# The value sums of the sample group's cached attention: weights held in the array and cached values moved through it, in place of the other way round

## The chip, the core and the metric

The kernel runs on one core of a Trainium2 chip. The time is that of one execution on the device, in microseconds (us); the profile is of another execution of the same program, taken by the hardware profiler. TensorE (PE) multiplies: a matmul has a stationary operand that is loaded first (PEld) and a moving operand that is then passed through it, column by column. VectorE (DVE), ScalarE (ACT) and GpSimd (POOL) work on elements; SyncE (SP) issues all DMAs of this kernel. PE writes to PSUM, which has eight banks of 512 fp32 numbers in each of 128 partitions.

## What is computed

The reference is one inference step of a decoder trunk with two layers (DEPTH = 2), for a prompt of 1024 tokens and for 8 sample sequences of one new token each. Half of each layer's 16 heads are window attention in three patterns (window, dilation), and for the sample group these heads read 2048 cached positions:

```
def dilated_gather_stats(q, k_all, v_all, window, dilation, buf_len):
    ...
    kg = jnp.take(k_all, idxc, axis=1).astype(jnp.float32)
    vg = jnp.take(v_all, idxc, axis=1).astype(jnp.float32)
    s = jnp.einsum('bthd,btjhd->bthj', q.astype(jnp.float32), kg) * (HEAD_DIM ** -0.5)
    ...
    o = jnp.einsum('bthj,btjhd->bthd', e, vg) / l[..., None]
    return m, l, o
```

The three patterns are merged by their softmax denominators. For each of 8 sequences b and 8 heads h the result is thus a sum over 3 x 128 cached values of 64 numbers, with one weight for each value, and over the new token's own value. The other eight heads are a matrix memory (mLSTM) that goes through the prompt in eight chunks of 128 tokens. Both halves are normalised, multiplied by w_out and added to x; then come a gated convolution block and a per-layer embedding.

## The kernel before

Each layer runs in stages: the input projection w_in in eight pairs of heads (`products`), each pair's projection lying beside the work of the pair before it; attention for pairs 0 to 3; the mLSTM for pairs 4 to 7; the output projection; the feed-forward block; the embedding. A hand-written order fixes what stands on each engine, and semaphores join the engines. Large products are made of three fp32r matmuls on split halves (lines 779 to 781); the small ones of attention and mLSTM are plain f32, and each of these shows as two matmul records in the trace.

The change lies in the last mLSTM pair (`q + 1 == PAIRS`), where no projection is left to lie beside it, and in what follows up to the output projection.

The mLSTM loop has eight steps c. On PE a step is: `sample_values(c)`; three products of the chunk (lines 1063, 1073, 1076); `kq(c + 1)` (line 994). On DVE it is: `finish(c)` (its first line is 1871, and it waits for PE's line 1076); `prepare(c + 1)`, which PE's lines 1063 and 1073 of the next step wait for; `output_gate(c)`; and a piece of the sample group's work: `sample_weights` at c = 0, `sample_turned` at 1, nothing at 2, `memory_gates` at 3, `memory_keys` at 4, `memory_output` at 5, `memory_update` at 6.

A tile i = 3b + r is 128 cached positions (pattern r of sequence b) by 512 numbers (8 heads by 64). `load_values(i)` brings one, `value_place(i)` is where it lies, in the space of the split operands `hi` and `lo` (trace name of the first: cache, of the second: vectors). The softmax weights are turned so that positions lie on partitions, and copied to `pT` (line 1764). At steps 2 to 7 `sample_values` takes four tiles each: for each quarter of a tile it loads 128 columns of values as the stationary operand and moves the 8 columns of weights (the 8 heads) of that b and r through it, which gives every head's weights times every value column (line 1011). Only the part with equal heads is wanted: eight copies of 8 columns pick it (`oT`, line 1936), before DVE normalises the first rows of y (`normalise`, line 1950).

After the loop, `normalise(t)` scales 128 tokens, `turn_y(t)` (line 1103) turns them on PE, `y_high` (ACT, line 1432) and `y_low` (DVE, line 1978) split them, and from t = 2 on the output projection can start. Behind its first product PE turns `oT` back (line 1089), DVE copies it to `so`, and two DMAs through DRAM bring it to the layout of `sv`.

SP issues DMAs in one order: 22 value tiles, then a wait for `rb_ready`, gains, half of X, two tiles of y, a store of the last output gate and a wait for it, its load, then tiles 22 and 23, each behind a count of `v_used`, then a wait for `mem_done` (the end of `memory_update`), the memory's stores and further y tiles.

## Time and profile before

| what | value |
|---|---|
| median of 3 runs | 3680.07 us (3679.55 to 3680.49) |
| the profiled execution | 3673.24 us, of it 3671.4 us from first to last instruction |
| PE busy | 3358.6 us (91%) |
| DVE busy | 2168.9 us (59%) |
| mean granted clock of PE | 0.934 of 2.4 GHz |

The table is of the whole run, and a change of one stage has to be read from that stage. The profile splits time by groups of instructions, by stretches (busy time of each engine and granted clock between two times), and in order of time. A granted clock of 1.00 is 2.4 GHz and one of 0.50 is 1.2 GHz. An engine's idle time stands in square brackets before the instruction that ended it, with what released it. Layer 1 of the two has the place in question at 770 to 852 us, layer 2 about 1803 us later.

### The profile page before, as it was taken

How to read it: one execution, taken by the hardware profiler on the slowest of the kernel's cores; microseconds unless marked ns; L12 is line 12 of the kernel's file. 1: busy time of each engine (PE TensorE's matmuls, PEld its weight loads, DVE VectorE, ACT ScalarE, POOL GpSimd, SP SyncE). 2: the span in 40 equal slices, each digit the busy share in tenths (PEclk: the TensorE clock that was granted, in tenths of full speed). 3: DMA queues.
4: the chain of work that ended last, by engine and by line, in shares of the span. 5: the costliest groups of instructions: out<-in, count | busy, mean ns of one | idle time of the engine just before them, and what ended most of it. 6: DMA issues, size and time to landing. Idle time of an engine off the chain costs nothing. (4 is left out here: it accounts for less than half of the span.)

```text
span 3671.4 us, 49568 instructions
## 1 busy us (share of the span) xinstructions
PE 3358.6 (91%) x19817; PEld 3084.5 (84%) x19817; DVE 2168.9 (59%) x4644; ACT 883.5 (24%) x1661; POOL 600.5 (16%) x498
## 2 busy tenths in 40 slices
PE   4888999988999999999978889997799999999989
PEld 4777767677899999998977777675798999999989
DVE  5566446657655555557566664566566555555573
ACT  4233223212311111113232323223032111111131
POOL 2001102110221221221110011111003221221211
PEclk7999989958999999999989999898599999999999
DMA  4111112343111111110211111134311111111101
GB/s 139 39 36 41 38 38 74 81 137 79 58 47 47 47 48 45 57 48 18 83 50 32 45 40 41 37 95 114 121 49 50 35 58 47 35 58 47 38 29 62
DMA packets 208269, 209.69 MB, mean 57 GB/s; under 512 B 34596, under 2 KB 180964, under 8 KB 205936
## 3 DMA queue, kind: packets, MB, share of 16 engines
q1 hardware_dynamic: 208040, 206.53, 18.7%
q8 instruction: 157, 2.57, 0.3%
q14 instruction: 72, 0.59, 0.1%
HBM read 175.03 MB, written 31.64 MB: 56 GB/s over the span
## 5 line engine op out<-in xcount | busy, mean ns | idle before, releaser
L763 POOL TENSOR_TENSOR wlo<-raw,whi 128x512 fp32r<-128x512 f32 (+3 forms) x488 | 599.8, 1264 | 3013.3 <-ACT whi L1251 3013.3
L779 PE MATMUL ps<-hi,wlo 128*128 128x344 f32 x2880 | 931.6, 323 | 25.7 <-DVE wb L2071 15.5
L780 PE MATMUL ps<-lo,whi 128*128 128x344 f32 x2880 | 925.0, 321 | 0.0
L781 PE MATMUL ps<-hi,whi 128*128 128x344 f32 x2880 | 924.6, 321 | 0.0
L779 PEld LDWEIGHTS ps<-hi,wlo 128*128 128x128 f32 x2880 | 546.2, 190 | 29.0 <-DVE wb L2071 16.1
L780 PEld LDWEIGHTS ps<-lo,whi 128*128 128x128 f32 x2880 | 545.5, 189 | 0.6
L781 PEld LDWEIGHTS ps<-hi,whi 128*128 128x128 f32 x2880 | 545.7, 189 | 0.0
L779 PE MATMUL ps<-whi,lo 128*128 128x512 f32 (+5 forms) x1152 | 463.0, 402 | 43.9 <-POOL wlo L763 25.6
L780 PE MATMUL ps<-wlo,hi 128*128 128x512 f32 (+5 forms) x1152 | 441.5, 383 | 0.0
L781 PE MATMUL ps<-whi,hi 128*128 128x512 f32 (+5 forms) x1152 | 441.3, 383 | 0.0
L2083 DVE TENSOR_TENSOR X<-X,ps 128x344 f32<-128x344 f32 x528 | 268.4, 512 | 196.1 <-PE ps L781 195.5
L779 PE MATMUL ps<-yhi,wlo 128*128 128x344 f32 x1056 | 339.8, 322 | 0.7 <-DVE X L2083 0.6
L781 PE MATMUL ps<-yhi,whi 128*128 128x344 f32 x1056 | 338.2, 320 | 0.0
L780 PE MATMUL ps<-ylo,whi 128*128 128x344 f32 x1056 | 337.3, 319 | 0.0
L779 PEld LDWEIGHTS ps<-whi,lo 128*128 128x128 f32 (+1 forms) x1152 | 216.6, 188 | 114.8 <-issue 58.4
L1477 ACT ACTIVATE wb<-wb 128x344 f32<-128x344 f32 x132 | 64.9, 492 | 848.9 <-DVE wb L2054 848.9
L781 PEld LDWEIGHTS ps<-whi,hi 128*128 128x128 f32 (+1 forms) x1152 | 215.7, 187 | 41.2 <-issue 3.6
L780 PEld LDWEIGHTS ps<-wlo,hi 128*128 128x128 f32 (+1 forms) x1152 | 216.6, 188 | 35.1 <-issue 3.0
L1251 ACT ACTIVATE whi<-raw 128x2048 fp32r<-128x2048 f32 (+3 forms) x122 | 214.0, 1766 | 52.1 <-DMA raw<-in_w_down 40.0
L1299 ACT ACTIVATE zt<-ps,rcol 128x256 f32<-128x256 f32 x144 | 68.0, 472 | 597.5 <-PE ps L781 460.6
L1705 DVE COPY att<-ps 128x512 f32<-128x512 f32 (+3 forms) x128 | 75.7, 591 | 221.6 <-PE ps L906 221.3
L779 PEld LDWEIGHTS ps<-yhi,wlo 128*128 128x128 f32 x1056 | 198.7, 188 | 2.1 <-DVE X L2083 1.5
(273 smaller groups left out, 4333.9 us busy)
## 6 DMA issues: line engine op xcount, KB each, us to landing
raw<-in_w_up SPq DMA_DIRECT2D x44, 1024.0 KB, 5.0
raw<-in_w_in SPq DMA_DIRECT2D x112, 256.0 KB, 4.4
raw<-in_w_down SPq DMA_DIRECT2D x22, 1024.0 KB, 4.7
kvb<-in_cache_win_k SPq DMA_DIRECT2D x48, 256.0 KB, 3.1
cache<-in_cache_win_v SPq DMA_DIRECT2D x36, 256.0 KB, 5.7
x_scratch<-X SPq DMA_DIRECT2D x8, 1032.0 KB, 6.9
X<-x_scratch SPq DMA_DIRECT2D x4, 2064.0 KB, 15.0
raw<-in_w_out SPq DMA_DIRECT2D x8, 1024.0 KB, 6.5
```

Source lines behind the costliest of these rows:

```text
L763: pool.tensor_tensor(out=wlo[:, s, r], in0=raw[:, s, r], in1=whi[:, s, r].bitcast(F32), op=ALU.subtract).then_inc(w_split, 1)
L779: nc.tensor.matmul(out, a_lo, b_hi, start=first, stop=False)
L780: nc.tensor.matmul(out, a_hi, b_lo, start=False, stop=False)
L781: return nc.tensor.matmul(out, a_hi, b_hi, start=False, stop=last)
L1251: do(nc.scalar.activation(whi[:, s, 0:used], raw[:, s, 0:used], ACT.Copy), w_hi, wait=False)
L1299: do(nc.scalar.activation(zt[0:m, z, t, 0:2 * P], src[:, 0:2 * P], ACT.Identity, scale=r), wait=False)
L1477: do(nc.scalar.activation(wb[:, col(c)], wb[:, col(c)], ACT.Gelu_apprx_tanh), gelu_done, wait=False)
L1705: do(v.tensor_copy(att[:, a:a + n], ps[:, 4, 0:n]), pt0, wait=False)
L2083: do(v.tensor_tensor(out=x, in0=x, in1=ps[:, 5 + g % 3, 0:CH], op=ALU.add), dn_read, wait=False)
```

## The change

The operands change places. A tile of values is now the moving operand, 512 columns; the stationary operand is 64 columns of `pZ`, one for each (b, h), in which only the 8 columns of this tile's b hold weights and the others are zero. So all 24 tiles add into one bank, 64 partitions (b, h) by 512 columns, with one matmul for a tile. `pZ` takes the place of three value tiles, so SP loads 19 tiles ahead and 5 behind counts of `v_used`. `pZ` is set to zero at the end of `sample_weights`, and `sample_turned` makes three copies with gaps in place of one. A table `heads` of zeros and ones (64 x 8, one more small DMA) picks the own head: one product of 64 x 512 out of PSUM, then a sum over heads straight into `sv`. Both stand right behind `normalise(0)`. The eight `oT` copies, the turn on PE, the copy to `so` and the two DMAs are gone; PE's third product of the output projection, which uses the same bank, waits for `so_done`.

```diff
         Cs, Ct = [lof[:, j * 2048:(j + 1) * 2048].rearrange("p (v k) -> p v k", k=HD) for j in (0, 1)]
         sm = lof[0:HD, 7168:7168 + 385]
-        pT = lof[:, 7560:7560 + 3 * HD]
+        pZ = lof[:, 5632:5632 + 3 * WA]
+        sown = lof[0:HD, 4096:4096 + WA].rearrange("p (h d) -> p h d", h=NH)
         zb = lof[0:HD, 7760:7760 + 3 * HD].rearrange("p (s d) -> p s d", s=3)
         small = lof[0:HD, 7960:7960 + 16]
 
...
         def value_place(i):
 
-            if 16 <= i < 22:
-                return lof[:, 4096 + (i - 16) * WA:4096 + (i - 15) * WA]
-            return hif[:, (i % 22) * WA:(i % 22 + 1) * WA]
+            s = i % 19
+            if s >= 16:
+                return lof[:, 4096 + (s - 16) * WA:4096 + (s - 15) * WA]
+            return hif[:, s * WA:(s + 1) * WA]
...
-                for i in range(22):
+                for i in range(19):
                     load_values(i)
                 sp.wait_ge(*at(rb_ready, 2 * PAIRS))
+                sp.dma_start(heads[:, :], A["c_heads"]).then_inc(ygain_in, 16)
                 for h, name in enumerate(("out_norm_a", "out_norm_b")):
                     sp.dma_start(rowr[:, h * WA:(h + 1) * WA], A[name][l:l + 1, :].to_broadcast([P, WA])).then_inc(ygain_in, 16)
                 sp.dma_start(X[:, 0:4, :], Xd[:, 0:4, :]).then_inc(x_back[0], 16)
...
                 sp.wait_ge(*at(z_stored[1], stored_value(last)))
                 sp.dma_start(mz[:, 2 * HD + 32:3 * HD], Zd[6].rearrange("b (r d) -> (b r) d", d=32)).then_inc(mo_in, 16)
-                for i in (22, 23):
-                    sp.wait_ge(*at(v_used, i - 21))
+                for i in range(19, 24):
+                    sp.wait_ge(*at(v_used, i - 18))
                     load_values(i)
                 sp.wait_ge(*at(mem_done, 1))
...
                 for t in (6, 7):
                     sp.wait_ge(*at(yt_ready, t - 3))
                     load_y(t)
-                sp.wait_ge(*at(so_done, 1))
-                sp.dma_start(Ad, so[:, :]).then_inc(as_stored, 16)
-                sp.wait_ge(*at(as_stored, 16))
-                sp.dma_start(sv[:, 1, :], Ad.rearrange("b (h d) -> (b h) d", d=HD)).then_inc(as_in, 16)
                 sp.wait_ge(*at(mh_stored, 32))
...
                         for i in range(4 * c - 8, 4 * c - 4) if c >= 2 else ():
                             b, r = divmod(i, 3)
+                            a = r * WA + b * HD
                             pe.wait_ge(*at(v_in[i // 6], 96))
-                            for x in range(4):
-                                mm = nc.tensor.matmul(ps[:, 6, x * HD + b * NH:x * HD + (b + 1) * NH], value_place(i)[:, x * P:(x + 1) * P],
-                                                      pT[:, r * HD + b * NH:r * HD + (b + 1) * NH],
-                                                      start=(r == 0 and x == 0), stop=(r == 2 and x == 3))
-                            mm.then_inc(v_used, 1)
+                            nc.tensor.matmul(ps[0:HD, 6, :], pZ[:, a:a + HD], value_place(i), start=(i == 0), stop=(i == 23)).then_inc(v_used, 1)
...
-                def turn_sample():
-
-                    pe.wait_ge(*at(ot_done, 1))
-                    for c in range(4):
-                        mm = nc.tensor.transpose(ps[0:NB, 7, c * P:(c + 1) * P], oT[:, c, :], ident[:, :])
-                    mm.then_inc(so_ready, 1)
...
-                        if j >= 3:
+                        if j == 2:
+                            pe.wait_ge(*at(so_done, 1))
+                        elif j >= 3:
                             pe.wait_ge(*at(wo_done, j - 2))
                         for k in range(KT):
                             w_h, w_l = weights(B + B_OUT + o // 2, k, 256, (o % 2) * P, P)
                             mm = three(ps[:, 4 + j % 3, 0:CH], w_h, w_l, hi[:, k, col(c)], lo[:, k, col(c)], k == 0, k == KT - 1)
                         mm.then_inc(gemm_done, 1)
-                        if c == 0 and o == 0:
-                            turn_sample()
                         if c == 0 and o + 3 < NT:
                             turn_y(o + 3)
                         if c == 1 and o == 3:
...
                     do(v.tensor_scalar(sv[:, 0, :], zb[:, 2, :], sm[:, 384:385], None, ALU.mult))
+                    do(v.memset(pZ, 0.0))
 
                 def sample_turned():
+
                     dve.wait_ge(*at(pj_back, 1))
-                    do(v.tensor_copy(pT, ps[:, 7, 0:3 * HD]), pj_done)
+                    for r in range(3):
+                        src = ps[:, 7, r * HD:(r + 1) * HD].rearrange("p (b h) -> p b h", b=NB)
+                        own = lof[:, 5632 + r * WA:5632 + r * WA + NB * (HD + NH)].rearrange("p (b x) -> p b x", b=NB)[:, :, 0:NH]
+                        do(v.tensor_copy(own, src), pj_done if r == 2 else None, wait=False)
...
                 rsqrt(yrs[:, :], yt2[:, :], ssq[:, :], WA, None)
-                dve.wait_ge(*at(v_used, 3 * NB))
-                for c in range(4):
-                    for e in range(2):
-                        r = slice(HD * e, HD * e + HD)
-                        src = ps[r, 6, c * 64:(c + 1) * 64].rearrange("p (b h) -> p b h", h=NH)[:, :, 2 * c + e]
-                        do(v.tensor_copy(oT[r, c, :], src), ot_done if (c, e) == (3, 1) else None, wait=False)
-                dve.wait_ge(*at(ygain_in, 32))
+                dve.wait_ge(*at(ygain_in, 48))
...
                 def sample_out():
-                    dve.wait_ge(*at(so_ready, 1))
-                    do(v.tensor_copy(so[:, :], ps[0:NB, 7, :]), so_done)
+
+                    dve.wait_ge(*at(v_used, 3 * NB))
+                    do(v.tensor_tensor(out=sown, in0=ps[0:HD, 6, :].rearrange("p (h d) -> p h d", h=NH),
+                                       in1=heads[:, :].unsqueeze(2).to_broadcast([HD, NH, HD]), op=ALU.mult), so_done)
 
                 def sample_sum():
-                    dve.wait_ge(*at(as_in, 16))
+                    do(v.tensor_reduce(out=sv[:, 1, :], in_=sown.rearrange("p h d -> p d h"), axis=AX.X, op=ALU.add))
                     do(v.tensor_tensor(out=sv[:, 0, :], in0=sv[:, 0, :], in1=sv[:, 1, :], op=ALU.add), sa_done)
...
                 normalise(0)
+                sample_out()
+                sample_sum()
                 for t in range(3):
                     normalise(t + 1)
                     if t == 0:
@@ -2008,10 +1997,6 @@
                             y_low(o + 3)
                         if c == 0 and o % 4 == 0:
                             dve.wait_ge(*at(x_back[o // 4], 16))
-                        if c == 0 and o == 1:
-                            sample_out()
-                        if c == 0 and o == 5:
-                            sample_sum()
                         if c == 1 and o == 1:
                             sample_norm()
                             normalise(NT)
...
-    return {"c_ident": ident, "c_mask": mask, "c_causal": causal, "c_rope": rope}
+    heads = np.equal(np.arange(HD)[:, None] % NH, np.arange(NH)[None, :]).astype(f)
+    return {"c_heads": heads, "c_ident": ident, "c_mask": mask, "c_causal": causal, "c_rope": rope}
```

On PE, in two steps of the loop over the last pair, before:

```order
L1011 MATMUL ps<-vectors,cache 128x8 x16
L1063 MATMUL ps<-zt,att 128x130
L1073 MATMUL ps<-zt,att 128x65 x2
L1076 MATMUL ps<-Cst,att 128x130
L994 MATMUL ps<-rstd,kT 128x128 x2
```

and with the change:

```order
L1007 MATMUL ps<-cache,vectors 64x512 x4
L1056 MATMUL ps<-zt,att 128x130
L1066 MATMUL ps<-zt,att 128x65 x2
L1069 MATMUL ps<-Cst,att 128x130
L990 MATMUL ps<-rstd,kT 128x128 x2
```

The 16 matmuls of four tiles became four, with 512 columns each in place of 8; nothing else of the step moved.

On DVE, between the end of the reciprocal root over all rows and the first split of y (vectors is the space where `sown` lies), before:

```order
L1548 TENSOR_TENSOR yrs<-yrs,yt 128x18
L1936 COPY oT<-ps 64x8 x8
L1950 SCALAR_TENSOR_TENSOR kvb<-kvb,yrs,rowr 128x512
L1950 SCALAR_TENSOR_TENSOR kvb<-kvb,yrs,rowr 128x384
L1950 SCALAR_TENSOR_TENSOR kvb<-yb,yrs,rowr 128x128
```

and with the change:

```order
L1534 TENSOR_TENSOR yrs<-yrs,yt 128x18
L1935 SCALAR_TENSOR_TENSOR kvb<-kvb,yrs,rowr 128x512
L1935 SCALAR_TENSOR_TENSOR kvb<-kvb,yrs,rowr 128x384
L1935 SCALAR_TENSOR_TENSOR kvb<-yb,yrs,rowr 128x128
L1942 TENSOR_TENSOR vectors<-ps,heads 64x512
L1946 TENSOR_REDUCE sv<-vectors 64x64
L1947 TENSOR_TENSOR sv<-sv 64x64
```

Eight short copies ahead of `normalise(0)` are gone, and three instructions stand between it and `normalise(1)`.

On SP, around the value tiles, before:

```order
L588 DMA cache<-in_cache_win_v 128x512 x16
L588 DMA vectors<-in_cache_win_v 128x512 x6
```

and with the change:

```order
L587 DMA cache<-in_cache_win_v 128x512 x16
L587 DMA vectors<-in_cache_win_v 128x512 x3
L657 DMA heads<-in_c_heads 64x8
```

The other three tiles went to where tiles 22 and 23 are loaded, behind the load of the last output gate.

## Rows read from the trace of the kernel before

**Rows 1.** The page's first line.

```profile
span 3671.4 us, 49568 instructions
```

**Rows 2.** Stretch: us, each engine's busy time (count), granted clock, DMA share, GB/s.

```profile
781.03:828.89 47.86, 47.72 (x220) 45.38 (x220) 28.69 (x75) 0.21 (x1) 0.00 (x0) 0.50 0.04 14
```

**Rows 3.** PE in order of time: start, duration, instruction, count; one step.

```profile
781.55 6.99 PE L1011 MATMUL ps<-vectors,cache 128*128 128x8 f32 x32
788.39 0.78 PE L1063 MATMUL ps<-zt,att 128*128 128x130 f32 x2
...
791.12 6.99 PE L1011 MATMUL ps<-vectors,cache 128*128 128x8 f32 x32
```

**Rows 4.** DVE in order of time: first line of `finish`, steps 1 to 7.

```profile
767.93 0.60 DVE L1871 SCALAR_TENSOR_TENSOR Cst<-Cst,cwb,ps 64x65 f32<-64x65 f32 x2 [1.63 <-PE ps L1076]
...
781.03 0.60 DVE L1871 SCALAR_TENSOR_TENSOR Cst<-Cst,cwb,ps 64x65 f32<-64x65 f32 x2 [9.12 <-PE ps L1076]
...
790.61 0.60 DVE L1871 SCALAR_TENSOR_TENSOR Cst<-Cst,cwb,ps 64x65 f32<-64x65 f32 x2 [6.28 <-PE ps L1076]
...
800.18 0.60 DVE L1871 SCALAR_TENSOR_TENSOR Cst<-Cst,cwb,ps 64x65 f32<-64x65 f32 x2 [4.06 <-PE ps L1076]
...
809.75 0.60 DVE L1871 SCALAR_TENSOR_TENSOR Cst<-Cst,cwb,ps 64x65 f32<-64x65 f32 x2 [2.92 <-PE ps L1076]
...
819.33 0.60 DVE L1871 SCALAR_TENSOR_TENSOR Cst<-Cst,cwb,ps 64x65 f32<-64x65 f32 x2 [2.89 <-PE ps L1076]
...
828.89 0.60 DVE L1871 SCALAR_TENSOR_TENSOR Cst<-Cst,cwb,ps 64x65 f32<-64x65 f32 x2 [0.95 <-PE ps L1076]
```

**Rows 5.** PE in order of time: 512-column f32 matmuls at either clock, and line 1063.

```profile
548.37 0.38 PE L1063 MATMUL ps<-zt,att 128*128 128x130 f32 x2
...
672.57 3.69 PE L1048 MATMUL ps<-rowr,ident 8*128 8x512 f32 x8
...
743.16 7.19 PE L1048 MATMUL ps<-rowr,ident 8*128 8x512 f32 x8
```

**Rows 6.** PE in order of time: two short runs at the lower clock.

```profile
358.92 2.93 PE L891 MATMUL ps<-zt 64*128 64x512 f32 x8 [2.75 <-DVE nm L1696]
...
496.10 3.17 PE L965 MATMUL ps<-ident,gz 128*8 128x128 f32 x16 [0.74 <-DVE yb L1713]
```

**Rows 7.** Stretches as in Rows 2: around those two runs, and two others.

```profile
358.90:362.10 3.20, 2.93 (x8) 1.17 (x8) 3.03 (x8) 0.99 (x2) 0.00 (x0) 0.50 0.26 82
362.30:366.00 3.70, 3.70 (x28) 3.66 (x29) 1.67 (x4) 1.59 (x4) 0.00 (x0) 1.00 0.00 0
...
495.30:498.60 3.30, 2.56 (x13) 1.52 (x13) 2.73 (x6) 0.00 (x0) 0.00 (x0) 0.50 0.29 84
498.80:502.00 3.20, 3.20 (x18) 2.64 (x16) 2.58 (x5) 0.00 (x0) 0.00 (x0) 1.00 0.66 238
...
743.20:750.30 7.10, 7.10 (x10) 2.44 (x8) 1.58 (x3) 2.18 (x8) 0.00 (x0) 0.50 0.97 75
851.70:857.00 5.30, 5.24 (x18) 5.24 (x19) 1.46 (x4) 0.00 (x0) 0.00 (x0) 0.50 0.60 53
```

**Rows 8.** The page's DMA issues: count, KB each, median us to landing.

```profile
cache<-in_cache_win_v SPq DMA_DIRECT2D x36, 256.0 KB, 5.7
```

**Rows 9.** Groups of DVE instructions: busy time and mean ns; or shortest, median, longest ns.

```profile
L1843 DVE TENSOR_TENSOR att<-ps,causal 128x512 f32<-128x512 f32 x32 | 20.6, 686 | 3.5 <-PE ps L1048 3.1
...
L1814 DVE MEMSET kT<- x2: 912/912/912, 497.9 to 2300.7; 8x1024 f32 x2
```

**Rows 10.** In order of time, behind the loop: DVE and PE.

```profile
838.92 1.52 DVE L1936 COPY oT<-ps 64x8 f32<-64x8 f32 x8
...
844.90 1.29 DVE L1978 TENSOR_TENSOR lo<-ps,hi 128x512 fp32r<-128x512 f32 x2 [1.43 <-ACT hi L1432]
...
842.16 3.64 PE L1103 MATMUL ps<-ident,kvb 128*128 128x128 f32 x16 [11.98 <-DVE kvb L1950]
...
858.05 0.60 PE L1089 MATMUL ps<-ident,oT 128*8 128x128 f32 x4
```

More of the change, by code:

```diff
@@ L210 @@
 PER = dict(
-    w_hi=NBLK, w_split=NBLK * PIECES, gemm_done=GEMM_ALL, vec_in=32, x_spilled=64, x_back0=16, x_back1=16, ygain_in=32,
+    w_hi=NBLK, w_split=NBLK * PIECES, gemm_done=GEMM_ALL, vec_in=32, x_spilled=64, x_back0=16, x_back1=16, ygain_in=48,
     split_hi=72, split_lo=72, sq_ready=72, sq_used=72, ss_ready=9, rstd_done=9, rcol_ready=3, rcol_done=3,
@@ L218 @@
     c_stored=192, zb_in=48, mz_in=208, mo_in=16, kq_used=24, st_ready=1, sp_max=1, sp_exp=1, pj_ready=1, pj_back=1, pj_done=1,
-    k_in0=192, k_in1=192, v_in0=96, v_in1=96, v_in2=96, v_in3=96, q_in0=64, q_in1=64, v_used=24, ot_done=1, so_ready=1, so_done=1,
-    as_stored=16, as_in=16, sc_exp_in=1, sc_exp=1, sa_done=1, sa_stored=16, mem_done=1, mh_stored=32, cst_in=16, cst_out=48,
+    k_in0=192, k_in1=192, v_in0=96, v_in1=96, v_in2=96, v_in3=96, q_in0=64, q_in1=64, v_used=24, so_done=1,
+    sc_exp_in=1, sc_exp=1, sa_done=1, sa_stored=16, mem_done=1, mh_stored=32, cst_in=16, cst_out=48,
     ys_in=48, yt_ready=9, yn_done=9, yh_done=18, yl_done=18, yst_in0=32, yst_in1=32, yst_in2=32, yst_in3=32, wo_done=24,
@@ L318, in build @@
         sv = sb("sv", [HD, 2, HD], F32, mid)
-        oT = sb("oT", [P, 4, NB], F32, mid)
-        so = sb("so", [NB, WA], F32, mid)
+        heads = sb("heads", [HD, NH], F32, mid)
         mz = sb("mz", [P, 3 * HD], F32, mid)
@@ L353, in build @@
         Hd = nc.dram_tensor("h_scratch", [NB, WA], F32).ap()
-        Ad = nc.dram_tensor("a_scratch", [NB, WA], F32).ap()
         ident_in, const_in, const_set = sem("ident_in"), sem("const_in"), sem("const_set")
@@ L390, in build @@
         q_in = [sem(f"q_in{s}") for s in range(2)]
-        v_used, ot_done, so_ready, so_done, as_stored, as_in, sc_exp_in, sc_exp = [sem(n) for n in (
-            "v_used", "ot_done", "so_ready", "so_done", "as_stored", "as_in", "sc_exp_in", "sc_exp")]
+        v_used, so_done, sc_exp_in, sc_exp = [sem(n) for n in ("v_used", "so_done", "sc_exp_in", "sc_exp")]
         sa_done, sa_stored, mem_done, mh_stored = sem("sa_done"), sem("sa_stored"), sem("mem_done"), sem("mh_stored")
```

## Prediction

> **What bounds the kernel now.** I read three views of the last mLSTM pair of layer 1: busy time by stretch, then PE and DVE in order of time. The stretch from `finish(2)` to `finish(7)` is 47.86 us; PE is busy for 47.72 of them and DVE for 28.69, at a granted clock of 0.50, the 1.2 GHz level [rows 2]. So PE sets the pace, and PE alone. A step is 9.57 us: 6.84 from the first matmul of four value tiles to line 1063 (781.55 to 788.39), and 2.73 for the chunk's products and `kq` (788.39 to 791.12) [rows 3]. The 6.99 us for 32 records are 0.218 each for 8 moving columns: what takes this time is the load of 128 columns, not the moving. DVE's first line of `finish` waits for PE in each step, by 9.12, 6.28, 4.06, 2.92, 2.89 and 0.95 us [rows 4]. Step lengths less these waits are what DVE itself needs: 9.58 - 6.28 = 3.30 us from `finish(2)` to `finish(3)`, then 9.57 - 4.06 = 5.51, 9.57 - 2.92 = 6.65, 9.58 - 2.89 = 6.69 and 9.56 - 0.95 = 8.61. Whatever PE gives back, a step can't go below these. Behind the loop the order turns: PE waits 11.98 us for `normalise` [rows 10], and DVE sets the end.
>
> **The matmuls.** Four tiles take four f32 matmuls, 8 records, of 512 columns. The nearest row is line 1048, also f32 and 512 columns: 8 records in 7.19 us at the low clock and in 3.69 us at the high one [rows 5], with one last pipeline tail in each; between starts I count 0.85 and 0.43. So four tiles cost 6.8 us at 1.2 GHz, what they cost now, and 3.4 us at 2.4 GHz. The exchange of operands gains nothing by itself. All hangs on the clock.
>
> **The clock.** Rows that speak for a rise: eight f32 records of 512 columns ran at 0.50 from 358.92, and the clock was 1.00 at 362.30; they were pairs of 64-row matmuls, two heads side by side [rows 6, 7]. Sixteen f32 records of 128 columns, with all 128 rows in use but only 8 stationary columns, ran at 0.50 from 496.10, and it was 1.00 at 498.80 [rows 6, 7]. So few stationary columns do not keep it down, and the new form (128 rows, 64 stationary columns, 512 moving) lies between those two. Against it: line 1048 kept PE busy for 7 us and the clock stayed at 0.50 [rows 7]. Its rows are 8 of 128, which the new form's aren't. Now, PE passes few columns in these steps, and the clock never moves. I take it that the clock rises about 3 us (3.4 and 2.7 in the two cases) after step 2's value tiles start, and holds: behind it PE is busy for 4.9 us of each step of 5 to 8.6.
>
> The Trainium skill, TensorE: Matmul & The Clock Gate, PE-mode transpose, says the full clock does not engage for transposes, since they do not count as busy in the same way. Line 965 is a transpose, and the clock rose behind it, so the trace does not bear this rule out here. The same page, Back-to-back issue gap, gives N / 1.2 ns at the cold clock, 427 ns for 512 columns; an estimate by that page would be 1.7 us for four tiles even without a rise, and DVE would then bound all steps and the gain would be near that of the forecast. The f32 rows show 0.85 us a record and two records a matmul, so the sum does not go by it.
>
> **The loop, per layer.** At the high clock a PE step is 3.4 + 2.73 / 2 = 4.8, with a little for hand-overs 4.9 us (line 1063 shows the halving: 0.78 us at the low clock, 0.38 at the high) [rows 3, 5]. A step is the longer of PE's and DVE's: 4.9, 5.51, 6.65, 6.69, 8.61, together 32.4 us, against 47.86: 15.5 less. Before `finish(2)`, step 2's tiles run 3 us at the low clock and the rest in half the time, and the products halve: 1.9 + 0.7 = 2.6 less if it is quick, nothing if the clock rises just behind the step; I take 1.9. Setting `pZ` to zero: 1536 columns at the rate of line 1814 (1024 in 0.912) are 1.4 us [rows 9], up to twice that beside POOL's work; it stands ahead of `finish(1)`, which now waits 1.63 us for PE [rows 4], so 0 to 1.2 shows; I take 0.4. Three copies of 64 columns in place of one of 192 are 0.3 us more, and PE waits for them. Loop: 15.5 + 1.9 - 0.7 = 16.7 less.
>
> **Behind the loop, per layer.** Eight `oT` copies, 1.52 us [rows 10], are gone from DVE's path, and `normalise(0)` comes 1.5 earlier. Added behind it: a product of 64 x 512 out of PSUM, 0.69 as line 1843 [rows 9], a sum with a stride, bounded by 0.5 and 1.4, taken as the product's 0.69, and an add, 0.2: 1.6 us. They shift `normalise(1)` back to where it was, but the first `y_low` waits 1.43 us today for ACT [rows 10], which waits for the first turn on PE; that turn is now earlier, so this wait closes. What is late next is `y_low(1)`, by the same turn: I count 1.1 less at the first product of the output projection, between -0.5 and 1.5. Line 1089's turn, 0.60 us with its tail [rows 10], goes from a PE-bound stretch: 0.4. The `so` copy, two DMAs and the earlier `sv` were waited for by nobody. Sum: 1.5 less.
>
> **SP.** Tiles 19 to 23 wait for counts 1 to 5 of `v_used`; the fifth comes early in step 3. Their landing takes 5.7 us each in the median [rows 8], and step 6 needs them some 17 us later (three steps): no cost. Queued behind these waits is only the wait for `mem_done`, which ends later. The memory's stores and the y tiles then start with `mem_done`, which comes right ahead of `finish(7)` where it came 0.95 us ahead; the y tiles are thus up to 0.9 nearer to their use. I cost that at nothing, at most 0.9. `heads` is 2 KB, long there.
>
> **Sum.** (16.7 + 1.5) x 2 = 36.4 us less. On the profiled execution's 3673.2 us (its span is 3671.4 [rows 1]) that is 3636.8; the median lies 6.8 above the profiled execution, so 3643.7. Unknown within it: where the clock stands when the output projection starts (it runs at 0.50 for 5.3 us now [rows 7], half of which can be gained or added, 2.7 a layer), the stretch before `finish(2)` (+0.7, -1.9), the zeroing (+0.4, -0.8), the tail (+0.4, -1.6). Taken together, not all at one end: 3634 to 3652.
>
> **Rivals.**
> 1. The clock stays at 1.2 GHz, since only 8 of 64 loaded columns are not zero, or by what keeps it down in line 1048. Then the loop is as now (6.8 against 6.84 for four tiles), less the 0.7 of added DVE work, and only the tail is won: 2 x (1.5 - 0.7) = 1.6 less, 3678.5. For: nothing has raised it in these steps so far. Against: lines 891 and 965. If transposes did not count, as the page has it, half of this evidence would fall, and this is the case that it would lead to.
> 2. The clock rises but falls back once DVE is the bound and PE waits some 2 to 3 us in steps 5 to 7, and steps run partly at the low clock. A step on PE at the low clock is 9.57, against 6.65 to 8.61 for DVE: 1 to 3 lost for each such step, 3 to 4 for steps 3 and 4. Three to five of them in each layer are 4 to 9 us: 3652 to 3662.
> 3. Slower: the clock stays low, and the weight loads are not hidden behind moving columns of the same rows. A load of 128 columns is 0.218 us [rows 3], one of 64 between half and all of that; 48 of them in each layer are 10 to 21 us over both layers. Taking the upper, 3678.5 + 21 = 3699.5. It decides from 0.08 us shown on each record (48 x 2 x 0.08 = 7.7 us). Against: the records of line 1048 stand end to end with their loads beneath them.
> 4. The change doesn't do what it says to PE's wait: tiles 19 to 23 come late and PE waits for them in step 6, up to 10 us a layer: 3645 to 3664.
>
> **How the numbers follow.** Forecast 0.74, rival 1 0.10, rival 2 0.10, rival 3 0.03, rival 4 0.03. Predicted: 3643.7. The range reaches from 3634 over rival 2 to 3662: 0.86 less what the forecast has outside its own bounds. A measurement of this kernel can tell about 0.2%, 7.4 us, from no change. Faster: forecast, rivals 2 and 4: 0.87. Same: rival 1: 0.10. Slower: 0.03.
>
> **What would show it.** The value matmuls at 0.85 us a record at first and 0.43 behind step 2; the granted clock 1.00 from step 3; DVE without waits from `finish(4)` on, 32 us from `finish(2)` to `finish(7)`; DVE idle less than 0.3 us before the first `y_low`. A clock of 0.50 through the stretch would prove the forecast wrong, and steps of over 10 us with it would mean rival 3.

## The result

The changed kernel takes 3643.22 us in the median of four runs (3641.94 to 3645.54), the kernel before, run beside it, 3680.28 us (3679.55 to 3680.98). The ratio is 0.9896, with a 95% interval of 0.9884 to 0.9908: 37.1 us less. Forecast were 3643.7 us and 36.4 us less.

The profiled execution of the changed kernel took 3642.27 us:

```profile
span 3640.5 us, 48964 instructions
PE 3315.6 (91%) x19521; PEld 3007.9 (83%) x19521; DVE 2170.7 (60%) x4636; ACT 883.6 (24%) x1661; POOL 600.6 (16%) x498
```

PE is busy for 43.0 us less than before and DVE for about as long as before. The stretches, in layer 1, are those of [rows 2] and [rows 7] moved to the same instructions: from `finish(1)` to `finish(2)`, on to `finish(7)`, on to the first product of the output projection, then two parts of the second stretch. Columns: us, busy time of PE, PEld, DVE, ACT and POOL (count), granted clock, DMA share, GB/s.

```profile
772.93:784.77 11.84, 7.51 (x22) 2.88 (x22) 4.46 (x14) 0.00 (x0) 3.14 (x3) 0.61 0.90 350
784.77:817.51 32.74, 25.69 (x100) 11.36 (x98) 28.70 (x76) 0.21 (x1) 0.00 (x0) 0.93 0.13 41
817.51:839.33 21.82, 6.51 (x26) 4.89 (x26) 20.69 (x49) 3.58 (x6) 0.00 (x0) 0.50 0.84 233
777.72:782.00 4.28, 4.28 (x5) 1.21 (x6) 0.00 (x0) 0.00 (x0) 0.00 (x0) 0.50 0.97 408
782.40:812.80 30.40, 28.06 (x111) 12.66 (x109) 24.07 (x74) 0.21 (x1) 0.00 (x0) 1.00 0.17 57
```

The second row answers to [rows 2]: 32.74 us for 47.86, at a clock of 0.93 for 0.50. DVE does the same 28.7 us of work in it and is now the busier engine. The fourth and fifth row show the clock: 0.50 until 782, then 1.00. The value matmuls in order of time on PE (start, duration, engine, line, operation, count; in brackets the idle time before) answer to [rows 3]:

```profile
777.72 5.84 PE L1007 MATMUL ps<-cache,vectors 128*64 128x512 f32 x8 [4.33 <-DVE vectors L1755]
785.00 3.65 PE L1007 MATMUL ps<-cache,vectors 128*64 128x512 f32 x8
788.58 0.49 PE L1056 MATMUL ps<-zt,att 128*128 128x130 f32 x2
790.09 3.65 PE L1007 MATMUL ps<-cache,vectors 128*64 128x512 f32 x8
```

Four tiles take 5.84 us in step 2, across the rise, and 3.65 behind it, where they took 6.99; a step of PE is 790.09 - 785.00 = 5.09 us, where it was 9.57. DVE's first line of `finish` for steps 1 to 7, which answers to [rows 4]:

```profile
772.93 0.60 DVE L1862 SCALAR_TENSOR_TENSOR Cst<-Cst,cwb,ps 64x65 f32<-64x65 f32 x2
784.77 0.60 DVE L1862 SCALAR_TENSOR_TENSOR Cst<-Cst,cwb,ps 64x65 f32<-64x65 f32 x2 [7.10 <-PE ps L1069]
789.88 0.60 DVE L1862 SCALAR_TENSOR_TENSOR Cst<-Cst,cwb,ps 64x65 f32<-64x65 f32 x2 [1.82 <-PE ps L1069]
795.43 0.60 DVE L1862 SCALAR_TENSOR_TENSOR Cst<-Cst,cwb,ps 64x65 f32<-64x65 f32 x2
802.13 0.60 DVE L1862 SCALAR_TENSOR_TENSOR Cst<-Cst,cwb,ps 64x65 f32<-64x65 f32 x2
808.85 0.60 DVE L1862 SCALAR_TENSOR_TENSOR Cst<-Cst,cwb,ps 64x65 f32<-64x65 f32 x2
817.51 0.60 DVE L1862 SCALAR_TENSOR_TENSOR Cst<-Cst,cwb,ps 64x65 f32<-64x65 f32 x2
```

The waits of 4.06, 2.92, 2.89 and 0.95 us are gone. The bound has passed from PE to DVE at `finish(4)`, and DVE keeps it.

Where the time went, by the same instructions in both traces (the first column is from the start of one to the start of the next):

| stretch, us | before, layer 1 / 2 | after, layer 1 / 2 |
|---|---|---|
| `finish(0)` to `finish(2)` | 22.92 / 22.93 | 20.90 / 21.47 |
| `finish(2)` to `finish(7)` | 47.86 / 47.85 | 32.74 / 32.74 |
| `finish(7)` to first output product | 22.87 / 22.66 | 21.82 / 21.83 |
| sum | 93.65 / 93.44 | 75.46 / 76.04 |

That is 18.2 and 17.4 us less. The turn at line 1089 of the kernel before is gone too (0.44 us in each layer, start to start), and the output projection runs at the low clock for 4.3 us in place of 5.3 in layer 1, which is worth 0.5. Together 37.0 us by these terms, and 37.1 by the medians. The two spans differ by only 30.9, since the profiled execution of the kernel before was a quick one: it starts `finish(0)` of layer 1 at 758.11, the changed kernel at 763.87, with the same instructions on PE and DVE up to there. From `finish(0)` to the end the two traces differ by 36.7, so the terms explain the difference to 0.3 us.

### The profile page after: what moved, and what is told of

Same layout as the page of the kernel before. It is cut to its first block and busy times, and to the rows that moved or that the text cites. A ratio compares the mean times of both kernels' runs of the same rounds, so it can differ in the third digit from the quotient of the medians.

```text
span 3640.5 us, 48964 instructions
## 1 busy us (share of the span) xinstructions
PE 3315.6 (91%) x19521; PEld 3007.9 (83%) x19521; DVE 2170.7 (60%) x4636; ACT 883.6 (24%) x1661; POOL 600.6 (16%) x498
```

## Experiments: what raised the clock

**Fewer rows.** The theory of the prediction was that line 1048 left the clock at 0.50 because it uses 8 of 128 rows. Here each value matmul uses 32 rows, and 96 of the 128 positions of a tile are left out.

```diff
-nc.tensor.matmul(ps[0:HD, 6, :], pZ[:, a:a + HD], value_place(i), ...)
+nc.tensor.matmul(ps[0:HD, 6, :], pZ[0:32, a:a + HD], value_place(i)[0:32, :], ...)
```

> The changed kernel, but each value matmul uses only rows 0 to 31 of its tile: 96 of the 128 positions of a tile are left out of the sum. Instructions, columns and waits are the same as in the changed kernel. Theory (the clock rose because these matmuls use all 128 rows; line 1048, 512 columns on 8 rows, left it at 0.50): the granted clock stays at 0.50 from finish(2) to finish(7) in layer 1, the eight value records of each step stay 0.85 us apart, a step is about 9.6 us, and the time is that of the kernel before less the tail, 3676 to 3681 us. Rival (512 moving columns a matmul and a busy PE are enough, whatever the rows): clock 1.00 from the second step on, 3641 to 3646 us.

Measured: 3679.21 us, ratio to the kernel before 0.9993 (0.9984 to 1.0003). The stretch from `finish(2)` to `finish(7)`, then two rows of PE's first step in it:

```profile
791.51:840.35 48.84, 48.68 (x100) 19.43 (x100) 28.71 (x76) 0.21 (x1) 0.00 (x0) 0.50 0.06 23
```

```profile
792.05 7.08 PE L1007 MATMUL ps<-cache,vectors 32*64 32x512 f32 x8
799.07 0.80 PE L1056 MATMUL ps<-zt,att 128*128 128x130 f32 x2
```

The same instructions, with PE busy for 48.68 of 48.84 us, leave the clock at 0.50. The rows in use, and with them the positions that enter the sum, are the only difference, so the theory stands. The run also shows the exchange of operands without its clock: a stretch of 48.84 us against 47.86, that is a loss of 1.0, which the shorter tail gives back. So nearly all of the 37 us hangs on the clock.

**Half the rows.** The same edit with `0:64`; half the positions of a tile are left out.

> The changed kernel, but each value matmul uses only rows 0 to 63 of its tile: half the positions of a tile are left out of the sum. With 32 rows the clock stayed at 0.50 and the time was 3679.2 us; with 128 it rises and the time is 3643 to 3645 us. Theory (rows in use count, in proportion): 64 rows with a PE busy to 70% of a step count like 128 rows on a PE busy to 35%, and the clock stays at 0.50 or rises late: 3655 to 3681 us. Rival (there is a step between 32 and 64 rows, as the 64-row pairs of line 891 did raise it): as with 128 rows, 3641 to 3646 us.

Measured: 3678.16 us, ratio 0.9998 (0.9989 to 1.0007), and again 48.84 us at 0.50:

```profile
786.26:835.10 48.84, 48.68 (x100) 19.49 (x100) 28.70 (x76) 0.21 (x1) 0.00 (x0) 0.50 0.09 29
```

So 64 rows in a row of matmuls do not raise it either. Line 891, whose matmuls have 64 rows as well, did [rows 6, 7]; its matmuls are pairs with two heads side by side. That the pairing makes the difference fits, but no run here took the pairs apart.

**Fewer loaded columns.** Rival 1 of the prediction: that only 8 of the 64 loaded columns are not zero might keep the clock down.

```diff
-nc.tensor.matmul(ps[0:HD, 6, :], pZ[:, a:a + HD], value_place(i), ...)
+nc.tensor.matmul(ps[0:NH, 6, :], pZ[:, a + b * NH:a + (b + 1) * NH], value_place(i), ...)
```

> The changed kernel, but each value matmul loads only the 8 columns of its own sample in place of the 64 padded ones, and writes 8 rows: the sums of all eight samples fall on each other, so the outputs of the cached values are left out as such. Columns moved, rows in use and waits are the same. Theory (rows in use and moved columns raise the clock, not the number of loaded columns): the clock rises in the same place, behind step 2's tiles, and the time is 3642 to 3645 us. Rival (the loaded columns count, the padding with zeros buys the clock): clock 0.50 through the loop and 3676 to 3681 us.

Measured: 3640.70 us, ratio 0.9892 (0.9877 to 0.9907). The clock rises with 8 loaded columns as with 64, at 782.1:

```profile
777.30 5.98 PE L1007 MATMUL ps<-cache,vectors 128*8 128x512 f32 x8 [3.59 <-DVE vectors L1755]
783.21 0.49 PE L1056 MATMUL ps<-zt,att 128*128 128x130 f32 x2
```

The padding buys the sum in one bank, and not the clock. The Trainium skill, TensorE: Matmul & The Clock Gate, PE-mode transpose, has the full clock not engage for transposes; the prediction put line 965 against it, a transpose with 128 rows and 8 loaded columns behind which the clock rose. This run has the same rows and loaded columns and the clock rises too, but it is no transpose, so whether transposes alone would raise it is not shown here.

**The padding alone.** The kernel before with `pZ` as its moving operand: 64 columns move in place of 8.

```diff
-nc.tensor.matmul(ps[:, 6, x * HD + b * NH:x * HD + (b + 1) * NH], value_place(i)[:, x * P:(x + 1) * P],
-                 pT[:, r * HD + b * NH:r * HD + (b + 1) * NH], start=(r == 0 and x == 0), stop=(r == 2 and x == 3))
+nc.tensor.matmul(ps[:, 6, x * HD:(x + 1) * HD], value_place(i)[:, x * P:(x + 1) * P],
+                 pZ[:, r * WA + b * HD:r * WA + (b + 1) * HD], start=(i == 0 and x == 0), stop=(i == 23 and x == 3))
```

> The kernel before with the padded table alone: the values still stand in the array and 64 padded columns move in place of 8, so 32 records of a step load 128 columns and move 64. The sums, the turn on PE, the eight copies and the two DMAs behind the loop stay as before. Theory (the load of 128 columns sets the pace, 0.218 us each, and the moved columns lie beneath it; PE's rows are used but few columns move, so the clock stays): 32 records still take 7.0 us, clock 0.50 in the loop, and the time is 3680 to 3683 us with the zeroing added. Rival (eight times the moved columns raise the clock already): clock 1.00 in the loop, four tiles in 3.5 us and 3645 to 3650 us.

Measured: 3680.11 us, ratio 0.9998 (0.9988 to 1.0007).

```profile
789.47 7.09 PE L1012 MATMUL ps<-vectors,cache 128*128 128x64 f32 x32
796.35 0.75 PE L1064 MATMUL ps<-zt,att 128*128 128x130 f32 x2
```

Thirty-two records are 6.88 us from start to the start of what follows, 0.215 each, with eight times the moved columns. The load of 128 columns sets this pace, as the prediction read from [rows 3], and 64 moved columns are free beneath it. All 128 rows are in use here and PE is busy for 47.75 us of the 47.88 from `finish(2)` to `finish(7)`, and still the clock stays at 0.50. So full rows and a busy PE did not raise it by themselves; in the changed kernel, where it rose, 512 columns moved for each load. Whether the more moved columns or the fewer loads make the difference, no run took apart.

**The same work earlier.** Two matmuls that nobody needs, put in PE's 4.3 us wait ahead of step 2.

```diff
 elif c == 2:
+    pe.wait_ge(*at(v_in[0], 96))
+    for i in (0, 1):
+        nc.tensor.matmul(ps[0:HD, 6, :], ident[:, 0:HD], value_place(i), start=True, stop=True)
     pe.wait_ge(*at(pj_done, 1))
```

> The changed kernel with two more f32 matmuls of 512 columns and 128 rows in the 4.3 us that PE waits for DVE ahead of step 2's value tiles; their result is overwritten by the first value matmul. At the low clock they take 3.4 us and fit in the wait. Theory (the clock rises 3 to 6 us behind the start of full-row work, whatever the work is for): it rises 3 to 5 us earlier, most of step 2's tiles run at 0.43 us a record in place of 0.85, finish(2) comes 2 to 3 us earlier in each layer, and the time is 4 to 6 us less than the changed kernel, 3638 to 3641 us. Rival (the two matmuls end late and push step 2 back, or the clock doesn't follow them): 3643 to 3647 us.

Measured: 3637.49 us, ratio 0.9890 (0.9876 to 0.9903), lower than 3643.22 by 5.7, with intervals of the ratio that overlap. By stretches it is half hit. Layer 1, then layer 2:

```profile
774.71 3.67 PE L1004 MATMUL ps<-cache,ident 128*64 128x512 f32 x4
779.12 5.38 PE L1010 MATMUL ps<-cache,vectors 128*64 128x512 f32 x8 [0.73 <-DVE vectors L1758]
...
2556.94 3.67 PE L1004 MATMUL ps<-cache,ident 128*64 128x512 f32 x4
2561.35 3.65 PE L1010 MATMUL ps<-cache,vectors 128*64 128x512 f32 x8 [0.73 <-DVE vectors L1758]
```

In layer 2 the clock rose 4.1 us behind the first of the added matmuls, all of step 2's tiles ran at 0.43 us a record, and `finish(1)` to `finish(2)` was 9.64 us against 11.69. In layer 1 it rose only at 782.6, 7.9 us behind them, and the stretch was 11.37 against 11.84. Without added matmuls the same stretch is 10.24 to 11.84 us in the four profiles with this order of DVE's work (10.24 in layer 2 of the kernel "Product and sum later" below), so only layer 2 lies outside that spread. So full-row work can be moved ahead to raise the clock, but in one of the two places it came no earlier than it does by itself. What decides that is open.

## Experiments: what bounds the changed kernel

**The changed kernel again**, run beside the three kernels with the memory's pieces earlier.

> The changed kernel once more, as a measure for the three kernels beside it and for how far one profiled execution differs from the next. Expected: 3641 to 3646 us, the clock rising 4 to 6 us behind the start of step 2's value tiles in both layers, finish(2) to finish(7) 32 to 34 us.

Measured: 3645.25 us (3640.87 to 3649.35), ratio 0.9906 (0.9891 to 0.9921); the clock rose 5.8 and 5.2 us behind the start of the value tiles, `finish(2)` to `finish(7)` took 32.75 and 32.74 us.

**The memory's pieces one step earlier.** Each condition stands on one line with its call here and in the next cut.

```diff
-elif c == 3: memory_gates()
-elif c == 4: memory_keys()
-elif c == 5: memory_output()
-elif c == 6: memory_update()
+elif c == 2: memory_gates()
+elif c == 3: memory_keys()
+elif c == 4: memory_output()
+elif c == 5: memory_update()
```

> The changed kernel with the four pieces of the sample's memory (gates, keys, output, update) at c = 2 to 5 in place of 3 to 6. Theory (DVE sets the length of the last four steps now, PE that of the first): the first step has room of 1.8 us for the gates, the rest moves one step up, and finish(2) to finish(7) is 1.5 to 2 us shorter in each layer: 3 to 4 us less in all. Rival (what DVE gains is lost again to PE, ACT or the stores behind mem_done): within 1 us of the changed kernel.

Measured: 3642.26 us, 3.0 less than beside it the changed kernel, ratio to the kernel before 0.9899 (0.9885 to 0.9914). `finish(2)` to `finish(7)` is 820.43 - 789.47 = 30.96 us, 1.8 less, as expected. So DVE is the bound of the last steps.

**The memory's pieces in the wait of step 2.**

```diff
 elif c == 1:
     sample_turned()
-elif c == 3: memory_gates()
-elif c == 4: memory_keys()
-elif c == 5: memory_output()
-elif c == 6: memory_update()
+    memory_gates()
+    memory_keys()
+elif c == 2: memory_output()
+elif c == 3: memory_scale()
+elif c == 4: memory_update()
```

`memory_scale` is the first three of the four operations of `memory_update`, cut from it; the third is the product of 128 x 2048 (2.29 us).

> The changed kernel with gates and keys at c = 1, in the 7.1 us that DVE waits for PE in step 2, the output at c = 2, and the update in two pieces at c = 3 and 4. Theory (DVE's own work sets steps 4 to 7): they fall to PE's 5.1 us or near it, finish(2) to finish(7) is 28 to 29 us against 32.7, and the whole 7 to 9 us less, 3634 to 3637 us. Rival (the output piece waits for the gate value mo, loaded late in step 2, or the work in the wait delays step 2's own products): half of that or less, 3638 to 3644 us.

Measured: 3633.10 us, 12.2 less than the changed kernel beside it, ratio to the kernel before 0.9875 (0.9860 to 0.9890). The starts of `finish`, steps 2 to 7:

```profile
786.05 0.60 DVE L1864 SCALAR_TENSOR_TENSOR Cst<-Cst,cwb,ps 64x65 f32<-64x65 f32 x2 [1.05 <-PE ps L1069]
792.76 0.60 DVE L1864 SCALAR_TENSOR_TENSOR Cst<-Cst,cwb,ps 64x65 f32<-64x65 f32 x2
799.04 0.60 DVE L1864 SCALAR_TENSOR_TENSOR Cst<-Cst,cwb,ps 64x65 f32<-64x65 f32 x2
804.75 0.60 DVE L1864 SCALAR_TENSOR_TENSOR Cst<-Cst,cwb,ps 64x65 f32<-64x65 f32 x2
808.08 0.60 DVE L1864 SCALAR_TENSOR_TENSOR Cst<-Cst,cwb,ps 64x65 f32<-64x65 f32 x2
813.15 0.60 DVE L1864 SCALAR_TENSOR_TENSOR Cst<-Cst,cwb,ps 64x65 f32<-64x65 f32 x2 [1.77 <-PE ps L1069]
```

The loop is 27.10 us, 5.6 less, in both layers, and DVE's wait ahead of `finish(2)` has shrunk from 7.10 to 1.05: 11.3 of the 12.2 us are there. More than I expected, because PE runs ahead while DVE works through steps 3 to 5, and DVE then does the step of 808.08 - 804.75 = 3.33 us, below PE's 5.09, without a wait. A step is not the longer of the two engines' each time; what an engine has done ahead counts.

**The same order in the kernel before.** The same places for the pieces, in the kernel with the values in the array; `memory_scale` has only the first two operations here, and the product of 128 x 2048 stays with `memory_update` at c = 4.

> The kernel before (values in the array) with the memory's pieces at c = 1 to 4, as in the order that took some 10 us from the changed kernel. Theory (in the kernel before PE alone sets these steps and DVE has 0.95 to 9.1 us of room in each): no gain in the loop, within 1 us of the kernel before. Rival (the stores behind mem_done start earlier and that helps behind the loop, or the order is worth something by itself): 2 us less or more.

Measured: 3680.67 us, ratio 1.0004 (0.9995 to 1.0012).

```profile
789.67:837.50 47.83, 47.72 (x220) 45.37 (x220) 23.65 (x59) 0.00 (x0) 0.00 (x0) 0.50 0.10 35
```

DVE has 5.0 us less to do in the stretch and it is as long as before. Nearly the order that takes 12 us from the changed kernel is worth nothing without the change: the bound had not passed to DVE. Where that one product stands can't matter here, since DVE waits 1.56 to 6.28 us for PE ahead of each `finish` there.

**Product and sum later.** The product with the 0/1 table, the strided sum and the add, from behind `normalise(0)` to behind `y_low(2)`; `sown` moves to columns that are free then.

```diff
 normalise(0)
-sample_out()
-sample_sum()
 for t in range(3):
     normalise(t + 1)
     ...
     y_low(t)
+sample_out()
+sample_sum()
```

> The changed kernel with its product with the 0/1 table, strided sum and add moved from behind normalise(0) to behind y_low(2), where DVE waits 6.2 us for ACT in the changed kernel. Theory (these 1.95 us of DVE are on the way to the second and third turn, where PE waits 1.44 and 0.68 us): the first product of the output projection comes 1 to 2 us earlier in each layer, 2 to 4 us less in all. Rival (ACT's copies behind the turns set that stretch, the DVE work is hidden): within 0.5 us of the changed kernel.

What DVE does behind `normalise(0)` in the changed kernel, and what PE waits for:

```profile
829.00 0.68 DVE L1942 TENSOR_TENSOR vectors<-ps,heads 64x512 f32<-64x512 f32 x1
829.71 1.02 DVE L1946 TENSOR_REDUCE sv<-vectors 64x64 f32<-64x512 f32 x1
830.76 0.22 DVE L1947 TENSOR_TENSOR sv<-sv 64x64 f32<-64x64 f32 x1
```

```profile
829.23 1.94 PE L1089 MATMUL ps<-ident,kvb 128*128 128x128 f32 x8 [10.43 <-DVE kvb L1935]
832.61 1.97 PE L1089 MATMUL ps<-ident,kvb 128*128 128x128 f32 x8 [1.44 <-DVE kvb L1935]
```

Measured with the later place: 3640.27 us, ratio 0.9890 (0.9875 to 0.9904), 3.0 less than the changed kernel's 3643.22 and 5.0 less than its 3645.25 in the second comparison; the intervals of the ratios overlap, so the stretch has to decide. DVE in it:

```profile
830.02 0.34 DVE L1935 SCALAR_TENSOR_TENSOR kvb<-yb,yrs,rowr 128x128 f32<-128x128 f32 x1
831.79 1.29 DVE L1965 TENSOR_TENSOR lo<-ps,hi 128x512 fp32r<-128x512 f32 x2 [1.43 <-ACT hi L1418]
```

The wait of 1.43 us for ACT, which [rows 10] have before the first `y_low`, is back. `finish(7)` to the first product of the output projection is 21.3 us in layer 1 (817.33 to 838.65) and 21.1 in layer 2, for 21.8: only 0.5 and 0.7 of the 1.95 us are won. Both the theory (1 to 2) and its rival (nothing) missed; two thirds to three quarters of the work were hidden. The 3.0 and 5.0 us by the medians are more than these 1.2, and the stretch does not show the rest.

**Both orders together.**

> The memory pieces in the wait of step 2 together with the product, sum and add behind y_low(2). If both theories hold the gains add up, as they are in different stretches: 9 to 13 us less than the changed kernel, 3630 to 3635 us. If only one holds, the time is that of the better of the two alone.

Measured: 3629.84 us (3628.77 to 3635.07), ratio to the kernel before 0.9868 (0.9851 to 0.9884), 3.3 less than the first order alone and 15.4 less than the changed kernel beside it. The loop is 27.12 and 27.12 us. The gains add up. By the stretches they are 12.5 us (5.6 in each loop, 0.7 and 0.5 behind it), within what was expected; the medians, with a spread of 8.5 us in the four runs of the changed kernel, give more. This is the fastest kernel of the study.

**Filling both waits.** To that kernel, the two matmuls ahead of step 2 and these behind the last pair:

```diff
 pe.wait_ge(*at(ct_done, PAIRS))
+for i in range(10):
+    nc.tensor.matmul(ps[0:HD, 4, :], ident[:, 0:HD], value_place(i), start=True, stop=True)
```

> The kernel with both new orders (the memory's pieces in step 2's wait, product and sum behind y_low(2); 3629.8 us), with the two filling matmuls ahead of step 2 and ten more behind the last pair, where PE waits 10.4 us for normalise(0). Expected ahead of step 2: DVE is within 1.2 to 1.6 us of PE there, so at most that is won. Behind the loop, theory (a full-row PE keeps or brings the clock to 1.00 ahead of the turns): the turns take 1.0 us in place of 1.9 and the output projection starts at the high clock, where it now runs 4.3 us at 0.50: 2 to 4 us less in each layer, in all 3620 to 3627 us. Rival (the ten matmuls run at the low clock, end behind normalise(0) and push the first turn back): 3629 to 3635 us.

Measured: 3633.49 us, ratio 0.9882 (0.9867 to 0.9896), 3.6 more than without them, with intervals of the ratio that overlap. Theory missed, and the traces are as the rival has it:

```profile
813.39 11.70 PE L1084 MATMUL ps<-cache,ident 128*64 128x512 f32 x20 [2.34 <-DVE cT L1924]
825.02 1.97 PE L1094 MATMUL ps<-ident,kvb 128*128 128x128 f32 x16
829.71 1.97 PE L1094 MATMUL ps<-ident,att 128*128 128x128 f32 x8 [2.72 <-DVE att L1942]
```

```profile
813.39:819.20 5.81, 5.81 (x7) 1.65 (x8) 5.36 (x14) 0.00 (x0) 0.00 (x0) 0.50 0.94 337
819.40:829.40 10.00, 7.59 (x30) 3.32 (x28) 5.99 (x14) 2.39 (x4) 0.00 (x0) 1.00 0.47 191
829.60:839.70 10.10, 7.89 (x29) 7.50 (x30) 7.41 (x14) 1.20 (x2) 0.00 (x0) 0.50 0.15 47
```

The ten started 2.3 us late, behind `ct_done`, ran at 0.50 for their first 5.8 us, and ended at 825.02; the first turn came 15.0 us behind `finish(7)` in place of 11.7. Then the clock fell again in the wait of 2.72 us, and the output projection started at 0.50 all the same. The first two turns were quicker, which did not pay for it: `finish(7)` to the first output product is 23.79 and 22.56 us, for 21.10 and 21.32 without the fillers, 3.9 more in both layers.

Ahead of step 2 the fillers did what was expected of them: `finish(1)` to `finish(2)` is 10.21 and 10.22 us for 11.80 and 11.33, 2.7 less. The clock rose 1.9 and 3.6 us behind the first of them. So up to the first output product the sum is 1.2 us more. The rest of the 3.6 fits the clock behind it, which stayed at 0.50 for 5.9 and 5.6 us of the output projection in place of 3.6 and 3.0, half of which is lost; but without fillers behind the loop this time was 3.0 to 5.9 us, so that part can be chance. Fillers ahead of step 2 alone, in the kernel with both orders, were not run.

## Why the prediction was right, step by step

**The bound before.** PE alone set the steps: nearly the same order of DVE's work gained nothing in the kernel before and 12 us in the changed one.

**The exchange by itself.** Put at nothing; with the clock kept at 0.50 by fewer rows, it costs 0.2 us a step. The records are 0.85 us at 1.2 GHz, as line 1048 had it [rows 5], and four tiles took 7.0 us with the hand-over. The Trainium skill, TensorE: Matmul & The Clock Gate, Back-to-back issue gap, has N / 1.2 ns between matmuls of N columns at the cold clock, from which the prediction worked out an estimate of 1.7 us for the four. The records of this case show four times that: two for each matmul, and each twice as long. What the prediction hung on it, that DVE would then bound all steps, was misread: PE's 1.7 + 2.73 us would still be longer than DVE's 3.30 in the first.

**The clock.** It rose, and did not with fewer rows, as the theory had it. The time that it took was off. I took 3 us from the start of step 2's tiles, from two cases; it was 4.5 in layer 1 (777.72 to 782.2) and 5.6 in layer 2. Over seven profiles of kernels in which this work raised it, without added matmuls, it was 2.8 to 5.9 us. It held until 812.9, behind the last value tiles (they end at 809.3). So the clock did fall in the last step, as rival 2 had it, but where DVE sets the end and nothing hangs on PE.

**The steps.** `finish(2)` to `finish(7)`: forecast 4.9, 5.51, 6.65, 6.69, 8.61; measured 5.11, 5.55, 6.70, 6.72, 8.66. 32.74 us for 32.4. The PE step is 5.09 for 4.9, as four tiles take 3.58 from start to next start where I had 3.4, and the rest 1.51 where I had 1.37. Step lengths less waits, read from before, were exact to 0.05 us each. What the rule lacked came out in the experiments: it takes each step alone. It held here only because DVE's steps grow from one to the next.

**Before `finish(2)`.** Forecast 1.9 less for the clock and 0.7 more for added work: 1.2. Measured from `finish(0)`: 2.0 and 1.5 less. The clock's part, from the first value tile to `finish(2)`, is 2.0 and 1.4 (9.06 us became 7.05, and 9.07 became 7.65). But its pieces are others: the tiles gave only 1.1 and 0.5, since the rise came later, and the products behind them 0.9 in each, which I had worked out as 0.7 and then left out. The added work cost 0.25 where I had 0.7: `finish(1)` came 0.12 later behind PE's turn of the weights (2.87 us for 2.75), and the three copies took 0.49 us for the one of 0.36. The zeroing was as long as I worked out, never longer beside POOL's work (1.34 us in all 24 profiled cases), and ends right at `finish(1)`:

```profile
771.56 1.34 DVE L1747 MEMSET vectors<- 128x1536 f32 x1 [0.39 <-DVE sv L1746]
```

That the clock's part came out near 1.9 is luck, and that the whole loop came out at 16.7 too: the added work was less than forecast, and the PE step longer.

**The tail.** Product and add as forecast (0.68 and 0.22 us for 0.69 and 0.2); the strided sum was taken as the product's 0.69 and is 1.02, inside its bounds of 0.5 and 1.4. The first `y_low` waits for nothing now, as forecast. The first output product came 1.05 and 0.83 us earlier for 1.1. The turn's 0.4 is there.

**SP.** Tile 23's load was issued at 787.9, and PE shows no wait ahead of a value tile behind step 2. Rival 4 fell. **Rival 3**, exposed loads, fell too: PEld is busy for 11.36 of 32.74 us beneath PE.

**The sum.** Loop 17.1 and 16.6 us less for 16.7; the whole 37.0 for 36.4. The use of the median in place of the profiled execution mattered more than the error of any term: from the quick execution alone the forecast would have been 3636.8.

## What to carry to other kernels

Read what an engine needs in a step as the step's length less its wait, for both engines, before you make one of them faster: it tells how far the gain goes and where it ends, and it told it here to 0.4 us in 32.7. Then move the other engine's work into the wait that is left; almost the same order was worth nothing before the bound had passed over, and 12 us after. An operand order can be worth its place for the clock alone, even where it costs a little at the same clock (1.0 us a layer here), but check in the trace that the clock follows.

## What the runs showed of the chip

- The steps with 512-column f32 matmuls kept PE busy for 48.68 of 48.84 us and left the clock at 1.2 GHz where these matmuls used 32 or 64 of 128 rows. It rose to 2.4 GHz where they used all 128, with 64 loaded columns or with 8.
- Loading 128 columns for each 64 moved left it at 1.2 GHz with all rows in use (47.88 us from `finish(2)` to `finish(7)` at 0.50, PE busy for 47.75).
- The rise came 2.8 to 5.9 us behind the start of the same work, and 1.9 to 7.9 behind the first of the fillers, so profiles of one program differ by some us. `finish(0)` of layer 1 began between 758.1 and 769.2 us in profiles of kernels with the same program ahead of it. A change of a few us has to be read from stretches, not from one span.
- A DVE operation was held up by POOL until POOL's own operation had ended. Line 1875 (8 x 128, then 128 x 128) of the changed kernel, and the eight POOL operations beside it, 1.25 us each; layer 1, then layer 2:

```profile
765.96 0.20 DVE L1875 TENSOR_SCALAR zt<-zt 8x128 f32<-8x128 f32 x1
775.21 0.95 DVE L1875 TENSOR_SCALAR zt<-zt 128x128 f32<-128x128 f32 x1
766.08 9.99 POOL L759 TENSOR_TENSOR wlo<-raw,whi 128x512 fp32r<-128x512 f32 x8 [46.38 <-ACT whi L1237]
2549.94 0.96 DVE L1875 TENSOR_SCALAR zt<-zt 8x128 f32<-8x128 f32 x1
2549.48 10.02 POOL L759 TENSOR_TENSOR wlo<-raw,whi 128x512 fp32r<-128x512 f32 x8 [46.46 <-ACT whi L1237]
```

In layer 1 the first operation began ahead of POOL's and took 0.20 us; the one that began at 775.21, in POOL's last operation, ended at 776.16, 0.09 behind POOL's end at 776.07. In layer 2 the first began within POOL's first operation and ended 0.17 behind the end of that. In all 14 profiles it is the same: the 8 x 128 operation took 0.20 us in 11 places, where it began ahead of POOL's, and 0.94 to 1.31 us in the other 17, where it ended 0.10 to 0.24 us behind POOL's running operation. The delay comes once in each layer: where the first took 0.20 us, the later one took 0.95, and 0.21 or 0.22 otherwise. That is why `finish(0)` to `finish(1)` is 9.06 us in layer 1 and 9.78 in layer 2, and it is nearly made up by `finish(2)`.
